# Conformer stage of a two-block transformer kernel: the last conv chunk, the layer norm and the first output units in two token halves, with the norm's sums taken chunk by chunk

## The reference, cut to what matters

```
a, g = split(x @ w_in + b_in, 2)          # 1024 -> 2 x 1024
h = a * sigmoid(g)
h = depthwise causal conv over tokens, 31 taps, + conv_b
mu = mean(h); xc = h - mu                 # over the 1024 features of a token
y = xc * rsqrt(mean(xc * xc) + eps) * ln_g + ln_b
out = silu(y) @ w_out + b_out
```

## Time and profile before

| | |
|---|---|
| median of three runs | 1516.6 us (1516.14 to 1517.24) |
| the profiled execution's own time | 1515.13 us |
| its span, first to last instruction | 1513.2 us |
| granted TensorE clock, mean | 0.989 |
| busy shares of the span | PE 97%, DVE 63%, ACT 43%, POOL 15% |
| stage ain on PE | from about 952 us to 1096 us |
| norm, PE mostly idle | about 1096 us to 1115 us |
| aout on PE | 1115.26 us to 1160.80 us |

### The profile page before, as it was taken

One profiled execution on the slowest core, in us unless ns is written; L12 is line 12 of the kernel. 1 busy time (PEld: TensorE's weight loads), 2 busy tenths in 40 slices (PEclk: granted clock), 3 DMA queues, 4 the chain that ended last, 5 costly groups with the idle time before them and its releaser, 6 DMA issues.

```text
span 1513.2 us, 19955 instructions
## 1 busy us (share of the span) xinstructions
PE 1461.1 (97%) x6748; PEld 1190.5 (79%) x6748; DVE 959.9 (63%) x1347; ACT 658.0 (43%) x1066; POOL 227.2 (15%) x155
## 2 busy tenths in 40 slices
PE   5799999999999999999999999999869999999999
PEld 3488888888887888888888888787648888888887
DVE  7877675464555667777745745699888763544532
ACT  5344443242446665444423425888854322222210
POOL 4200000000202232000000005499702000000000
PEclk9899999999999999999999999999989999999999
...
GB/s 154 56 111 83 110 85 125 70 99 98 95 112 56 43 57 70 100 109 86 108 111 83 83 101 94 56 70 56 28 42 111 98 97 107 88 102 93 99 103 49
DMA packets 38956, 132.45 MB, mean 88 GB/s; under 512 B 4208, under 2 KB 4464, under 8 KB 38896
## 3 DMA queue, kind: packets, MB, share of 16 engines
...
## 4 chain that ended last, share of the span: by engine, by line
PE 84%; POOL 7%; ACT 5%; DVE 3%; issue 1%; DMA 0%; ACTq 0%; POOLq 0%; DVEq 0%
PE bank L482 27%; PE bank L484 26%; PE bank L483 26%; POOL prod L469 5%; POOL ssum L442 2%; PE bank L605 1%; ACT dgl L1029 1%; PE bank L633 1%; PE bank L618 1%; ACT dgh L1027 1%; ACT tapped L1042 1%; ACT whi L786 1%; PE bank L535 0%; PE bank L573 0%; PE bank L529 0%
## 5 line engine op out<-in xcount | busy, mean ns | idle before, releaser
L482 PE MATMUL bank<-xh,whi 128*128 128x512 f32 x1200 | 473.9, 395 | 1.4 <-DVE res L1366 0.7
L484 PE MATMUL bank<-xh,wlo 128*128 128x512 f32 x1200 | 467.1, 389 | 0.0
L483 PE MATMUL bank<-xl,whi 128*128 128x512 f32 x1200 | 467.0, 389 | 0.0
L786 ACT ACTIVATE whi<-raw 128x1024 fp32r<-128x1024 f32 (+1 forms) x248 | 258.3, 1043 | 234.4 <-PE bank L484 234.3
L1105 DVE TENSOR_TENSOR wlo<-raw,whi 128x1024 fp32r<-128x1024 f32 (+1 forms) x248 | 309.7, 1249 | 56.0 <-ACT whi L786 48.6
L482 PEld LDWEIGHTS bank<-xh,whi 128*128 128x128 f32 x1200 | 225.6, 188 | 52.5 <-issue 4.4
L483 PEld LDWEIGHTS bank<-xl,whi 128*128 128x128 f32 x1200 | 225.3, 188 | 49.6 <-issue 3.5
L484 PEld LDWEIGHTS bank<-xh,wlo 128*128 128x128 f32 x1200 | 225.3, 188 | 47.3
L482 PE MATMUL bank<-ahi,whi 128*128 128x512 f32 x608 | 236.5, 389 | 0.0
L483 PE MATMUL bank<-alo,whi 128*128 128x512 f32 x608 | 236.5, 389 | 0.0
L484 PE MATMUL bank<-ahi,wlo 128*128 128x512 f32 x608 | 236.5, 389 | 0.0
...
## 6 DMA issues: line engine op xcount, KB each, us to landing
...
```

Source lines behind the costliest of these rows:

```text
L482: nc.tensor.matmul(out_, hi, mh, start=first, stop=False)
L483: nc.tensor.matmul(out_, hi, ml, start=False, stop=False)
L484: return nc.tensor.matmul(out_, lo, mh, start=False, stop=last)
L786: nc.scalar.activation(whi[:, s, 0:tiles * P], raw[:, s, 0:tiles * P], ACT.Copy)\
```

## The change

Five things are changed together.

1. The first chunk's per-token mean over its 128 features (`shift_sum`, one matmul with ones) is subtracted from all of `hv`: from chunks 0 to 2 by three DVE instructions in chunk 3, from later ones by starting the DVE taps with `-mean` (kept in `rms`). So sums and sums of squares can be taken without the true mean, which is removed at the end (`offset`, `variance`).
2. Both sums of a chunk are taken on the way: ACT squares chunks 0 to 2 in its iteration 4 and chunk c - 2 in iterations 5 and 6, and PE's `feature_sums`, two matmuls with ones for each chunk, stand where `feature_sum` stood and wait for these squares.
3. The partial sum of the DVE taps moves from bank 5 (now needed for the sum of squares) into bank 6 or 7, the bank that `convolve` of the same chunk overwrites. So `convolve` now waits for the chunk's last DVE tap (`tap_steps`).
4. The last chunk's two chains, gate, taps and convolution, and the whole norm, are done in two halves of H = 256 tokens; centring moves to POOL (`hv - u`, 16 instructions of 256 columns).
5. In aout the first four units run interleaved, tile by tile, first for tokens 0 to 255, then for 256 to 511; units 4 to 7 follow one by one, each in two halves of 256 columns. Their weights go to the same four slots that units 0 to 3 hold until their last matmul. DVE's reciprocal of `r1` and the four `rescale` steps of `res` stand behind the norm of both halves and ahead of the evictions and of the split of unit 4.

The diff, cut to its core (`rescale` is L1136 of before, `add_out` is L1140 of before on a half or on all tokens; `scale_ln` and `lo_ln` are L1510 and L1513 on a half; `variance` is one DVE instruction, `invert_ln` a reciprocal, `join_sums` four DVE instructions, `activate` a silu and a rounding, `deviation` a root; `gate_last`, `last_hi`, `open_last`, `gated_last`, `last_lo`, `collect_last` are the steps of a chunk on a half):

```diff
+            def convolve(c, h=None):
...
+                if h is None:
+                    pe.wait_ge(tap_steps, own_steps(c + 1))
...
                 mm.then_inc(conv_done, 1)
-            def feature_sum(c):
-                pe.wait_ge(hv_ready, c + 1)
-                mm = nc.tensor.matmul(norm[0][:], ones[:], hv[:, c, :], start=(c == 0), stop=(c == C - 1))
-            for c in range(C):
...
+            def feature_sums(c, h=None):
+                at = slice(0, T) if h is None else cols(h)
+                pe.wait_ge(xcsq_ready, c + (h or 0) + 1)
+                first, last = c == 0 or h == 1, c == C - 1
+                nc.tensor.matmul(bank[7][:, 0:H] if h else norm[0][:, at], ones[:], hv[:, c, at], start=first, stop=last)
+                nc.tensor.matmul(bank[7][:, H:T] if h else norm[1][:, at], ones[:], square_at(c)[:, at],
+                                 start=first, stop=last).then_inc(sums_done, 1)
+            for c in range(C - 1):
                 if c == 0:
                     first_chains("ain", "ain")
                 for k in (2 * (c % 2), 2 * (c % 2) + 1) if c else ():
                     chain(p, c // 2, k, xh, xl)
                 if c >= 1:
                     convolve(c - 1)
-                if c >= 2:
-                    feature_sum(c - 2)
-            convolve(C - 1)
-            feature_sum(C - 2)
-            feature_sum(C - 1)
+                if c == 2:
+                    shift_sum()
+                for e in range(SHIFTED) if c == 4 else (c - 2,) if c >= 5 else ():
+                    feature_sums(e)
+            for h in range(2):
+                for j in range(2):
+                    at = acc[2 + j if h == 0 else j][:, 0:H]
...
+            convolve(C - 2)
+            feature_sums(C - 3)
+            convolve(C - 1, 0)
+            feature_sums(C - 2)
+            feature_sums(C - 1, 0)
+            convolve(C - 1, 1)
+            feature_sums(C - 1, 1)
             p = ph["aout"]
+            pe.wait_ge(lo_done, p.unit + SLOTS)
+            pe.wait_ge(acc_free, p.chain)
+            for h in range(2):
+                for t in range(C):
+                    pe.wait_ge(ln_lo, C * h + t + 1)
+                    for k in range(SLOTS):
+                        mm = three(bank[k + 4 * h][:, 0:H], whi[:, k, w], wlo[:, k, w], yhi[h][:, t, :],
+                                   ylo[:, t, cols(h)], t == 0, t == C - 1)
+            for k in range(SLOTS):
+                pe.wait_ge(lo_done, p.unit + SLOTS + k + 1)
+                pe.wait_ge(first_half_free, 2 + k + 1)
+                for h in range(2):
...
+            def square(c, h=None):
+                at = slice(0, T) if h is None else cols(h)
+                if c < SHIFTED:
+                    act.wait_ge(xc_ready, c + 1)
+                else:
+                    act.wait_ge(hv_ready, c + (h or 0) + 1)
+                if c >= 4:
+                    act.wait_ge(sums_done, c - 3)
+                nc.scalar.activation(square_at(c)[:, at], hv[:, c, at], ACT.Square).then_inc(xcsq_ready, 1)
...
+            def offset(h):
+                if h == 0:
+                    act.wait_ge(sums_done, C)
+                else:
+                    act.wait_ge(sums_joined, 1)
+                total = u[:, 3, cols(h)] if h else norm[0][:, cols(h)]
+                nc.scalar.activation(u[:, 0, cols(h)], total, ACT.Copy, scale=1.0 / D).then_inc(offset_ready, 1)
+                nc.scalar.activation(u[:, 1, cols(h)], total, ACT.Square, scale=1.0 / D).then_inc(offset_squared, 1)
...
-                if c == C - 1:
-                    products(c - 1, range(PARTS, POOL_TAPS[c - 1]))
+                for e in range(SHIFTED) if c == 4 else (c - 2,) if c >= 5 else ():
+                    square(e)
                 products(c, range(min(PARTS, POOL_TAPS[c])))
+                diagonals(c + 1)
+            gate_last(0)
+            last_hi(0)
+            products(C - 2, range(PARTS, POOL_TAPS[C - 2]))
+            square(C - 3)
+            products(C - 1, range(POOL_TAPS[C - 1]), 0)
+            gate_last(1)
+            last_hi(1)
+            products(C - 1, range(POOL_TAPS[C - 1]), 1)
+            split_hi(p.unit, 0, 2 * C - 2 + AHEAD)
             nc.scalar.activation(eps[:, 4:5], eps[:, 0:1], ACT.Sqrt)
+            square(C - 2)
+            split_hi(p.unit, 0, 2 * C - 1 + AHEAD)
+            square(C - 1, 0)
+            offset(0)
+            split_hi(p.unit, 0, 2 * C + AHEAD)
+            deviation(0)
+            for c in range(3):
+                activate(0, c)
+            square(C - 1, 1)
+            offset(1)
+            for c in range(3, 6):
+                activate(0, c)
+            deviation(1)
+            for c in range(6, C):
+                activate(0, c)
             for c in range(C):
+                activate(1, c)
+            p = ph["aout"]
             for c in range(C):
+                if c < C - 1:
+                    split_hi(p.unit, 0, c + SLOTS)
+                act.wait_ge(acc_free, p.chain + c + 1)
+                prepare("mlp", c, c % 2, ph["ain"].end_chain)
...
-            def own_tap(c, n, k):
-                x, w = hc[:, c % 2, k:k + T], v("conv_w", c * TAPS + k)
-                if n == 0:
-                    V.tensor_scalar(taps[:], x, w, None, ALU.mult).then_inc(tap_steps, 1)
+            def own_tap(c, n, k, h=None):
+                at, width = (0, T) if h is None else (h * H, H)
+                x, w = hc[:, c % 2, at + k:at + k + width], v("conv_w", c * TAPS + k)
+                part = bank[6 + c % 2][:] if h is None else acc[2 + h][:, 0:H]
+                done = own_steps(c) + n + (len(own_taps(c)) if h else 0)
+                if n == 0 and c < SHIFTED:
+                    V.tensor_scalar(part, x, w, None, ALU.mult).then_inc(tap_steps, 1)
                     return
+                if n:
+                    dve.wait_ge(tap_steps, done)
+                V.scalar_tensor_tensor(hv[:, c, at:at + width] if n == len(own_taps(c)) - 1 else part, x, w,
+                                       part if n else rms[:, at:at + width], op0=ALU.mult, op1=ALU.add)\
+                    .then_inc(tap_steps, 1)
...
+                if c == SHIFTED:
+                    dve.wait_ge(mean_done, 1)
+                    dve.wait_ge(hv_ready, SHIFTED - 1)
+                    for e in range(SHIFTED - 1):
+                        V.scalar_tensor_tensor(hv[:, e, :], norm[0][:], -1.0 / P, hv[:, e, :],
+                                               op0=ALU.mult, op1=ALU.add).then_inc(xc_ready, 1)
+                    V.tensor_scalar(rms[:], norm[0][:], -1.0 / P, None, ALU.mult).then_inc(shift_ready, 1)
+                    dve.wait_ge(shift_ready, 1)
...
+                if c == SHIFTED:
+                    dve.wait_ge(hv_ready, SHIFTED)
+                    V.scalar_tensor_tensor(hv[:, c - 1, :], norm[0][:], -1.0 / P, hv[:, c - 1, :],
+                                           op0=ALU.mult, op1=ALU.add).then_inc(xc_ready, 1)
+            c, late = C - 1, late_taps(C - 2)
+            own = own_taps(c)
+            open_last(0)
+            gated_last(0)
+            for n, k in enumerate(own):
+                if n == 4:
+                    last_lo(0)
+                own_tap(c, n, k, 0)
+            open_last(1)
+            gated_last(1)
+            for n, k in enumerate(own):
+                if n == 4:
+                    last_lo(1)
+                if n == 9:
+                    for m, e in enumerate(late):
+                        late_tap(c - 1, m, e)
+                    collect(c - 1)
+                own_tap(c, n, k, 1)
+            collect_last(0)
             split_lo(p.unit, 0, 2 * C - 2 + AHEAD)
+            variance(0)
             split_lo(p.unit, 0, 2 * C - 1 + AHEAD)
+            invert_ln(0)
+            scale_ln(0, 0)
+            split_lo(p.unit, 0, 2 * C + AHEAD)
+            scale_ln(0, 1)
+            collect_last(1)
+            lo_ln(0, 0)
+            scale_ln(0, 2)
+            lo_ln(0, 1)
+            scale_ln(0, 3)
+            lo_ln(0, 2)
+            join_sums()
+            scale_ln(0, 4)
+            variance(1)
+            for e in range(5, C):
+                scale_ln(0, e)
+                lo_ln(0, e - 2)
+            lo_ln(0, C - 2)
+            lo_ln(0, C - 1)
+            invert_ln(1)
+            for e in range(C):
+                scale_ln(1, e)
+                if e:
+                    lo_ln(1, e - 1)
+            lo_ln(1, C - 1)
+            V.memset(ssum[:], 0.0).then_inc(ssum_ready, 1)
+            V.reciprocal(r1[:], r1[:]).then_inc(rinv_ready, 1)
             dve.wait_ge(rinv_ready, 8)
+            p = ph["aout"]
+            for e in range(SLOTS):
+                rescale(e)
+            for e in range(SLOTS):
+                dve.wait_ge(first_half_done, 2 + e + 1)
+                add_out(e, cols(0), acc[e][:, 0:H], first_half_free)
+            for e in range(C):
+                if e < SLOTS:
```

(9 more changed lines are left out.)

273 lines of the change are left out of this document (169 added, 104 removed).

## The result

The changed kernel takes **1543.62 us** (median of four runs, 1543.04 to 1544.43), the kernel before 1516.92 in the same comparison (1516.14 to 1517.44): ratio 1.0177, 95% interval 1.0159 to 1.0194. It is 26.7 us slower. I had forecast 1532 with a range up to 1541: the direction was right, the size was not. The profiled execution took 1543.64 us, its span is 1541.7, 28.5 more than before's; before's profiled execution lay 1.8 us under its median.

What follows compares the result with a forecast made beforehand. PE was taken as full nearly everywhere, the conv loop balanced, the norm the only large hole. A last gate 12.0 us late, a tail giving back 4.8 and a longer aout made +15.3 us on 1516.6: 1532, range 1526 to 1539 (wider: 1519 to 1541).

Steps and rivals of the forecast that it cites:

- Part 1: convolve(0) waits for all its chunk's DVE taps: starts 5.0 us later, PE 6.5 us late with a 1.5 us restart.
- Part 2: Shift by the first chunk's mean: DVE reaches chunk 4 some 4.2 us late, gate(4) at 1031.0, not 1026.78.
- Part 3: PE's sums before chunk 5's chains wait for ACT's squares: PE idles 5.9 us, gate(5) 1055.8, lag 12.0 us.
- Part 4: Tail, last gate to aout: PE sets it without pause; 27.9 us in place of 32.7, halves give back 4.8.
- The port: DVE's scalings and first taps collide with POOL's centrings and product sums; five collisions make 1537 us; chance 0.10.
- My two signs of being wrong: Either gate(7) lies before 1088, or PE passes from the interleaved units to unit 4 without a pause.
- Part 5: aout: PE stands 4.5 us before unit 4, whose split is late on DVE; ends at 1176.1 against 1160.80.
- PE keeps its lead: Loop iterations 4 to 6: squares ready when PE comes, only the sums' own time paid; total 1519; chance 0.15.

Runs made afterwards that it cites:

- E2: Changed kernel with DVE's partial sums of chunks 0 to 2 back in bank 5 and no wait for taps in their convolutions: 1541.39 us.
- E5: Changed kernel with four edits together (PE's sums one iteration later, early partial sums in bank 5, collect earlier in DVE's tail, r1 early): 1530.40 us.
- E1: Changed kernel with PE's feature sums in the loop one iteration later, behind the next chains, ACT's squares unmoved: 1535.56 us.
- E9: Changed kernel with the last 4 of chunk 7's 13 DVE taps left out in both halves: 1538.29 us.
- E3: Changed kernel with collect of chunk 6 and collect_last(0) placed earlier in DVE's list of the last chunk: 1540.28 us.
- E8: Changed kernel with POOL's 16 centrings left out, DVE's scalings waiting for the offset instead: 1540.44 us.
- E13: Changed kernel, halves kept: later sums, no shift, moved partial sums, earlier collect, early r1, reordered second half: 1527.96 us, 15.3 behind a full-width kernel without shift (1512.71).

## Why the prediction was wrong in size

| from | before | forecast | measured |
|---|---|---|---|
| lateness of the last gate | 0 | +12.0 | +13.45 |
| last gate to aout's first matmul | 32.7 | 27.9 | 35.65 |
| aout to the first chain behind it | 45.5 | 53.6 | 57.54 |
| sum | | +15.3 | +28.4 |

**Part 1** held in place (974.53 for 974.2), and E2 shows how little of it passes on. Its last sentence, that later chunks' taps are done before PE comes, held only because PE was late: with PE ahead again E5 waits 6.4 us for the taps of chunk 3. **Part 2** held: gate(4) at 1031.90 for 1031.0. **Part 3**, the dearest term, held: first sums 1037.76 for 1036.8, chains 1045.31 for 1044.1, gate(5) 1057.55 for 1055.8, the pause 5.30 for 5.9. E1 confirms its mechanism.

**Part 4 failed, with the step "PE is without a pause there, so PE sets this stretch."** It was 7.75 us too short. I added up PE's matmuls and then ran the first half's norm behind them, but never laid DVE's list from gate(7) on beside it. PE's own list was right: it ended the first half of `convolve(7)` at 1111.15, for 1109.8 and 1.4 us of later gate. Then came the pause of 3.98 us and a slow start. From the last gate to `offset` (1119.58) went 23.55 us where I had 17.9, 5.65 of the 7.75; from there to aout 12.1 where I had 10.0. DVE's list holds 26 taps of half width, which I had priced nowhere, and `collect` of chunk 6 behind nine taps of the second half. What the runs put in its place: DVE sets the stretch (E9, 5.3 us for eight taps), its order makes PE pause (E3), and POOL's centring doubles its scalings (E8). The port, which I had as a rival at 0.10, is a term of 3.2 us inside the case that came, 2.1 of them in this stretch. My two signs of being wrong did not look at this stretch, and neither came; what gave the error away was aout's first matmul, at 1131.68 where I had named 1122.

**Part 5** had the mechanism (the idle time before unit 4, released by `wlo`) and mis-sized it by 3.9 us. Of the 57.5 us 46.0 are 384 matmuls at 0.12. The pauses are 1.51 + 5.00 = 6.5 us where I had 4.5, and what is left for two restarts and short gaps is 5.0 where I had 3.0: unit 4's restart alone is 28 matmuls from 1163.72 to 1169.59, 0.21 us apart instead of 0.12, 2.5 us for my 1.5.

The rival on the other side, PE keeps its lead, did not come; its mechanism is E1's, and it would have given 8.1 us, not enough for the sign.

Argued only: how E13's 15.3 us divide between the gate, the pauses and the half-width matmuls; no run took them out one by one. E5 shows besides that gains measured singly don't add up, so the differences in the table of runs are not shares of the 28.4 us.
